# Half as many key columns in the second attention mixer: query heads in another order

## What is computed

```python
DSA_SIZES = (1024, 256, 256, 256, 32, 8)          # q, k, v, qi, ki, wi
def mixer_dsa(x, w_in, w_out):                    # x: 256 x 1024, w_in: 1024 x 1832
    q, k, v, qi, ki, wi = jnp.split(x @ w_in, DSA_SPLITS, axis=-1)
    q = q.reshape(Bn, S, 4, 4, 64)                # 16 heads of queries, 4 share one head of keys
    k = k.reshape(Bn, S, 4, 64)
    v = v.reshape(Bn, S, 4, 64)
    def block(q_b, qi_b, wi_b, bid):              # 128 positions
        rel = relu(einsum('bqhd,bsd->bqsh', qi_b, ki))
        score = einsum('bqsh,bqh->bqs', rel, wi_b) * idx_scale    # causal mask, then the top 64
        _, idx = lax.top_k(score, 64)
        logits = q_b . k[idx] / 8 - slopes[head] * distance       # masked softmax over them
        return (softmax(logits) . v[idx]).reshape(Bn, 128, 1024)
    return concat(blocks) @ w_out
```

## Time and profile before

| | |
|---|---|
| median of 3 runs | 3656.43 us (3653.99 to 3658.11) |
| the profiled execution | 3654.87 us, its span 3653.6 us |
| mean granted TensorE clock | 0.821 of full |
| PE busy over the span | 2616.1 us (72%) |
| DVE, POOL, ACT busy | 2061.5, 1516.7, 518.2 us |
| records of L1256 on BIG | 576 |

### The profile page before, as it was taken

One profiled execution on the slowest core, in us unless ns is written; L12 is line 12 of the kernel. 1 busy time (PEld: TensorE's weight loads), 2 busy tenths in 40 slices (PEclk: granted clock), 3 DMA queues, 4 the chain that ended last, 5 costly groups with the idle time before them and its releaser, 6 DMA issues.

```text
span 3653.6 us, 35023 instructions
## 1 busy us (share of the span) xinstructions
PE 2616.1 (72%) x12888; PEld 1202.7 (33%) x12888; DVE 2061.5 (56%) x5112; ACT 518.2 (14%) x1007; POOL 1516.7 (42%) x1609
## 2 busy tenths in 40 slices
PE   6688777755556865655588585556665889899998
PEld 1233222111112321111154221112312575767765
DVE  0367777656667667866404577666898354231411
ACT  1121011100012111100022110001210122020200
POOL 0035556546666666666500156666566210000000
PEclk8889888788667887767789687776867899999999
DMA  8789999999999999999822599998999786667577
GB/s 308 257 310 363 357 393 379 403 401 389 366 350 364 385 367 354 337 361 366 310 104 81 208 364 391 363 366 333 393 358 347 263 303 223 207 256 253 216 246 263
DMA packets 363672, 1156.36 MB, mean 317 GB/s; under 512 B 33712, under 2 KB 33968, under 8 KB 362476
## 3 DMA queue, kind: packets, MB, share of 16 engines
q0 software_dynamic: 232144, 849.51, 61.4%
q1 hardware_dynamic: 130940, 304.36, 23.2%
q10 hardware_dynamic: 416, 0.23, 0.0%
HBM read 1152.84 MB, written 1.15 MB: 316 GB/s over the span
## 4 chain that ended last, share of the span: by engine, by line
PE 39%; DVE 21%; DMA 20%; POOL 8%; issue 7%; another core or an unknown queue 3%; ACT 2%; SPq 0%; DVEq 0%; ACTq 0%; POOLq 0%
DMA BIG<-in_p_v_dram,IDX 12%; POOL BIG L2363 8%; PE PS L1158 8%; DVE BIG L1959 8%; PE PS L1092 7%; PE PS L1380 6%; PE PS L1362 6%; DMA BIG<-in_p_u_dram,IDX 4%; PE PS L1256 2%; PE PS L1350 2%; DMA WR<-in_w_mod_dram 1%; PE PS L1120 1%; DVE SC L2157 1%; DVE I L1883 1%
## 5 line engine op out<-in xcount | busy, mean ns | idle before, releaser
L1158 PE MATMUL PS<-BIG,DG 64*64 64x512 f32 x6144 | 1057.6, 814 | 674.0 <-DMA BIG<-in_p_v_dram,IDX 500.4
L2363 POOL DMA_INDIRECT BIG<-in_p_u_dram,IDX x768 | 735.1, 957 | 1021.4 <-ACT SCU L1525 242.5
L1959 DVE CUSTOM_DVE_ANT_0 BIG<-BIG,PS 128x1024 f32<-128x1024 f32 x768 | 927.9, 1215 | 312.7 <-DMA BIG<-in_p_u_dram,IDX 272.9
L2363 POOL DMA_INDIRECT BIG<-in_p_v_dram,IDX x768 | 738.6, 962 | 345.7 <-issue 180.4
L1158 PEld LDWEIGHTS PS<-BIG,DG 64*64 64x64 f32 x6144 | 274.4, 168 | 1342.3 <-issue 1220.1
L1092 PE MATMUL PS<-WR,HT 128*128 128x512 f32 x640 | 297.8, 619 | 10.0 <-DMA WR<-in_a_w_in_dram 4.6
L1362 PE MATMUL PS<-HT,WR 128*128 128x128 f32 x2048 | 259.8, 288 | 5.5 <-DVE mv L1807 4.9
L1362 PEld LDWEIGHTS PS<-HT,WR 128*128 128x128 f32 x2048 | 251.0, 203 | 15.5 <-issue 8.9
L1380 PE MATMUL PS<-WR,BIG 128*128 128x512 f32 x512 | 226.2, 597 | 0.0
L1092 PEld LDWEIGHTS PS<-WR,HT 128*128 128x128 f32 x640 | 123.5, 198 | 177.2 <-issue 168.5
L1380 PEld LDWEIGHTS PS<-WR,BIG 128*128 128x128 f32 x512 | 97.1, 192 | 117.4 <-issue 117.1
(11 more groups left out here) (320 smaller groups left out, 2714.0 us busy)
## 6 DMA issues: line engine op xcount, KB each, us to landing
WR<-in_mlp_w_dram SPq DMA_DIRECT2D x128, 1024.0 KB
WR<-in_w_mod_dram SPq DMA_DIRECT2D x48, 1024.0 KB
WR<-in_b_w_in_dram SPq DMA_DIRECT2D x18, 1024.0 KB
WR<-in_a_w_in_dram SPq DMA_DIRECT2D x16, 1024.0 KB
WR<-in_p_w_q_dram SPq DMA_DIRECT2D x16, 1024.0 KB
BIG<-in_dsa_w_dram POOLq DMA_DIRECT2D x16, 1024.0 KB, 7.6
BIG<-in_p_u_dram,IDX POOLq DMA_INDIRECT x768
BIG<-in_p_v_dram,IDX POOLq DMA_INDIRECT x768
```

What stands on the lines that cost most here:

```text
L1158: mm = self.e.matmul(pv[64 * i:64 * i + 64, 2 * r + n, :], dg[p, :], row[p, n * 512:n * 512 + 512], start=h == 0 and j == 0, stop=h == 7 a ...
L1959: self.e.tensor_tensor_reduce(row, row, xp, 1.0, 0.0, ALU.mult, ALU.add, m.ACTV[:, u % 4, j:j + 1]).then_inc(*self.done("dot", l, u, j))
L2363: self.e.indirect_dma_start(row, None, m.A[f"p_{table}"], bass.IndirectOffsetOnAxis(ap=m.IDX[:, u % 4, j:j + 1], axis=0)).then_inc(*m.GR.l ...
```

## The change

The 16 query heads get the order `DSA_ORDER` = 0, 4, 1, 5, 2, 6, 3, 7, 8, 12, 9, 13, ... An even place then always holds a head that uses key head 0 (or 2), an odd place one that uses key head 1 (or 3), so a tile with key head 0 on partitions 0 to 63 and key head 1 on 64 to 127 serves all of the first eight. The host permutes the query columns of `dsa_w` and the rows of `dsa_w_out_2` accordingly, and no longer repeats the keys. The keys' slab has 256 columns, its two pieces are 512 KB each, and `column` is called twice for it instead of four times. In the list of arrays of `layout` `dsa_w_out_2` moves from before `p_u` to behind `dsa_w`. The core of the diff:

```diff
+DSA_ORDER = [8 * (s // 8) + 4 * (s % 2) + s % 8 // 2 for s in range(16)]
...
-        self.side_slab(("dsa_v", b), w, 1536)
-        self.side_slab(("dsa_i", b), w, 2048, 136)
-
-    def columns(self, slab, rhs, dst, after, pace=1):
-        for i in range(4):
-            self.column(slab, i, rhs, dst, after)
+        self.side_slab(("dsa_v", b), w, 1280)
+        self.side_slab(("dsa_i", b), w, 1792, 136)
+
+    def columns(self, slab, rhs, dst, after, pace=1, count=4):
+        for i in range(count):
+            self.column(slab, i, rhs, dst, after, count)
             yield from beats(pace)
...
         for n, dst in ((2, m.d_k[:, :, b * 128:(b + 1) * 128]), (0, m.d_q[:, 0:4, :]), (1, m.d_q[:, 4:8, :])):
-            self.side_slab(("dsa", b, n), w, n * 512)
+            self.side_slab(("dsa", b, n), w, n * 512, 512 if n < 2 else 256)
             yield from beats(2)
-            yield from self.columns(("dsa", b, n), self.block_of(b), dst, ())
+            yield from self.columns(("dsa", b, n), self.block_of(b), dst, (), count=4 if n < 2 else 2)
...
-        self.e.matmul(ps[:, 0:n], m.d_q[p, h // 2, :], m.d_k[p, h // 4, 0:n], start=True, stop=True).then_inc(
+        self.e.matmul(ps[:, 0:n], m.d_q[p, h // 2, :], m.d_k[p, h // 8, 0:n], start=True, stop=True).then_inc(
...
-        m, kv = self.m, h // 4
+        m, kv = self.m, DSA_ORDER[h] // 4
...
-        self.e.scalar_tensor_tensor(lg, m.d_nd[:, 0:n], 2.0 ** (-8.0 * (h + 1) / 16), m.d_mn[:, 0:n], ALU.mult,
+        self.e.scalar_tensor_tensor(lg, m.d_nd[:, 0:n], 2.0 ** (-8.0 * (DSA_ORDER[h] + 1) / 16), m.d_mn[:, 0:n], ALU.mult,
```

More of the change, by code:

```diff
@@ L237, in __init__ @@
         self.s_end = sb("s_end", [128, 2, 16])
-        self.d_k, self.d_q = (flat[:, 1024 * i:1024 * i + 1024].rearrange("p (h t) -> p h t", h=4 + 4 * i)
-                              for i in range(2))
+        self.d_k = flat[:, 0:512].rearrange("p (h t) -> p h t", h=2)
+        self.d_q = flat[:, 1024:2048].rearrange("p (h t) -> p h t", h=8)
         self.d_score, self.d_nd, self.d_mn, self.d_ki = (flat[:, 2048 + 256 * i:2304 + 256 * i] for i in range(4))
@@ L1247, in inter, with column @@
                       skip_group_check=True).then_inc(*self.done("inter", h, j, n))
-    def column(self, slab, i, rhs, dst, after):
+    def column(self, slab, i, rhs, dst, after, count):
         m = self.m
@@ L1255, in column @@
             self.wait_ge(m.side.landed(slab, k // 4))
-            mm = self.e.matmul(ps[:, i * 128:(i + 1) * 128], self.side_of(slab, k)[:, i * 128:(i + 1) * 128], rhs(k),
+            mm = self.e.matmul(ps[:, i * 128:(i + 1) * 128], self.side_of(slab, k, count * 128)[:, i * 128:(i + 1) * 128], rhs(k),
                                start=k == 0, stop=k == 7)
         mm.then_inc(*self.done("cols", slab))
-        if i == 3:
+        if i == count - 1:
             for k in range(2):
@@ L1630, in coefficients, with column @@
         self.e.activation(x1, x1, ACT.Sin).then_inc(*self.done("sines"))
-    def column(self, slab, i, rhs, dst, after):
+    def column(self, slab, i, rhs, dst, after, count):
         m = self.m
-        if i < 3:
+        if i < count - 1:
             return
+        ps = m.PS.of("cols", slab)[:, 0:128 * count].rearrange("p (i t) -> p i t", i=count)
         self.wait_ge(m.pe.at("cols", slab))
-        self.e.activation(dst, m.PS.of("cols", slab).rearrange("p (i t) -> p i t", i=4), ACT.Copy).then_inc(
-            *self.done("cols", slab))
+        self.e.activation(dst, ps, ACT.Copy).then_inc(*self.done("cols", slab))
         m.PS.free(("cols", slab), self.done.last())
@@ L2554, in layout @@
               "b_gn_g", "b_w_out", "p_w_q", "sb_ssm_w_in_2", "ssm_w_glu_2",
-              "sb_ssm_w_out_2", "dsa_w_out_2", "ln_mix_g_2", "ln_mix_b_2", "ln_ffn_g_2", "ln_ffn_b_2",
+              "sb_ssm_w_out_2", "ln_mix_g_2", "ln_mix_b_2", "ln_ffn_g_2", "ln_ffn_b_2",
               "mlp_w1_2", "mlp_w2_2"):
@@ L2560, in layout @@
     w = a["dsa_w_in_2"][0]
-    k = np.repeat(w[:, 1024:1280].reshape(1024, 4, 1, 64), 2, axis=2).reshape(1024, 512)
+    q = w[:, 0:1024].reshape(1024, 16, 64)[:, DSA_ORDER].reshape(1024, 1024)
     ki = np.repeat(w[:, 1792:1824].reshape(1024, 1, 32), 4, axis=1).reshape(1024, 128)
-    o["dsa_w"] = c(np.concatenate([w[:, 0:1024], k, w[:, 1280:1792], ki, w[:, 1824:1832]], axis=1))
+    o["dsa_w"] = c(np.concatenate([q, w[:, 1024:1280], w[:, 1280:1792], ki, w[:, 1824:1832]], axis=1))
+    o["dsa_w_out_2"] = c(a["dsa_w_out_2"].reshape(1, 16, 64, 1024)[:, DSA_ORDER].reshape(1, 1024, 1024))
     w = np.zeros((33, 2, 512), np.float32)
```

## The result

The changed kernel has a median of 3637.38 us over 10 runs (3626.19 to 3647.97), beside 3655.21 us over 10 runs of the kernel before on the same chips (3642.96 to 3665.15). The ratio is 0.9954, with a 95% interval of 0.9938 to 0.997: 17 us faster, between 11 and 23. On another chip, where the kernel before takes 3522.98 us, a second set gave 3509.64 us, ratio 0.9961 (0.9945 to 0.9977), 13 us. The forecast was 15.2 us.

The account below looks back on a forecast made before the run. The prediction took PE to bound the tail, with gather waits ahead of it untouched. Its terms, 7.1 + 3.7 + 4.4 = 15.2 us, off the 3656.43 us median gave 3641 us, with a range from 3635 to 3650.

Parts of the forecast that it names:

- Term 1: Work removed from PE in the tail: two key column groups fewer per block, four at 1.79 us each, saving 7.1 us.
- Term 2: PE's 5.9 us of waits for the keys' slab: smaller pieces land sooner, saving 3.7 us (bounds 2.0 to 5.9).
- Term 3: PE's low clock behind the key waits: 2.8 us regained in block 0, 1.6 in block 1, together 4.4 (bounds 0 to 6.0).
- The waits cost more than their length: Step claiming that behind the key waits PE runs at 1.2 GHz instead of 2.4; low level priced at 2.8 and 3.2 us.
- The second query slab's cover: Time between that slab's landing and PE's need of it, expected to shrink from 6.9 us to over 2 us.
- Columns only: Rival: the key waits move elsewhere or stay with the clock low, so only 7.1 us is gained, 3649.3; chance 12%.
- The gathers by address: Rival: moving dsa_w_out_2 shifts the row tables and PE's gather waits grow; with 5% growth slower, 3666 us; chance 6%.
- The late slab: Rival: the second query slab lands 3.0 us late, costing 6 us per block, leaving a gain of 3, 3653; chance 7%.

Follow-up runs that it names:

- e2: Changed kernel with key pieces loaded 512 columns wide (1 MB), only 256 used, two column groups: tail 539.83 us, ratio 0.9978.
- e3: Changed kernel with each key group made twice (four groups), pieces still 512 KB: tail 543.40 us, ratio 0.999.
- e5: Changed kernel, unchanged, profiled a second time, on a second chip: tail 536.61 us, ratio 0.9961 to the kernel before.
- e7: Changed kernel with dsa_w_out_2 back in its old place in the host's list: tail 536.78 us, ratio 0.9963 to the kernel before.
- e4: Kernel before, same work; first query slab issued right behind the keys, key groups four beats behind their issue instead of two: tail 543.73 us, ratio 0.9972.
- e12: Changed kernel with the second query slab's groups begun at the beat of its issue instead of two beats behind: tail 539.36 us, ratio 0.9957.
- e11: Kernel before (512 key columns, 1 MB pieces) with key groups three beats behind their issue instead of two: tail 538.62 us, ratio 0.9975.
- e10: The kernel of e4, unchanged, profiled a second time on another chip: tail 541.90 us, ratio 0.999 to the kernel before.
- e6: Kernel before with only dsa_w_out_2 moved behind dsa_w in the host's list: tail 549.95 us, ratio 0.9999.

## Why the prediction held, and where its terms were off

**What bounds the kernel.** The tail is PE's: it is busy for about 94 to 95% of it in every profile, and groups put in or taken out moved the end by their price (e2, e3).

**Term 1, 7.1 us, is right.** There are 64 records fewer, the 32 matmuls of four groups, and e3 puts them back for 6.6 to 7.8 us.

**Term 2, 3.7 us, was too small by about one.** The landing of the first pieces was right to 0.3 us (5.1 and 4.7 against 4.95 and 4.45). Of 5.9 us of waits 1.6, 0.7 and 0.8 are left in the three profiles, so 4.3 to 5.2 are saved. What the step missed is that PE reads the keys when it gets there, and in block 0 of the first profile it got there later than computed, since the slow stretch ahead of them was longer in that execution (3.78 us for the MLP group instead of 3.46). In e5 and e7, where it was not (3.51 and 3.47), 0.5 to 0.7 us were waited there, as forecast, but the clock fell ahead of the keys of block 1 and left 0 and 0.3.

**Term 3, 4.4 us, was too large, and its reason fell.** PE's busy time is 8.2 to 10.0 us shorter, of which 7.2 are groups: the clock gave 1.0 to 2.9. A small part was the price: the prediction took 1.04 us, a row of L1079, for a half group at full clock, and rows of L1257 at 1.00 have 1.16, so its bound of 6.0 was 0.5 too high. The step that failed is "The waits cost more than their length": it read the slow groups behind the waits as caused by them. In block 1 of the first profile after it looks like that: the clock stayed up. But the order of e4 took all waits for the keys away and got 0.4 us from the clock in one execution and 3.1 in another, e2 had 2.7 us of waits in block 0 without a fall, and in e5, e7 and e3 the fall in block 1 came back as a slow group behind the first index head, and one more in the heads. That the waits have no part in it is not shown either: in all three profiles of the kernel before the clock is low behind both pairs of waits, and in e12 behind one of 1.71 us. What ties the falls to their places stays open. The kernel before shows the same slow groups, to about 0.1 us, in three executions on three chips; the order of e4 shows different ones in two; e11, which changes nothing but the beats, has 7.7 us less busy time in its one execution.

The Trainium skill, "TensorE: Matmul & The Clock Gate", Part 1, has the moment of the change depend on a free-running monitor, with other counts of slow matmuls from run to run. The pairs e4 and e10 (busy 516.48 and 513.81) and after and e5 (506.84 and 508.64) agree with that, though each pair is from two chips; the three profiles of the kernel before (516.78 to 516.87), and e5 and e7 on one chip (508.64 and 508.66), do not show it.

**The sum.** 7.2 + 4.3 to 5.2 + 1.0 to 2.9 gives, profile by profile, 13.3 to 14.5 us in the tail, against 15.2: the errors of terms 2 and 3 had opposite signs. That the sum is off by only 0.7 to 1.9 us is therefore in part luck. The 17 us measured on the first chip, with an interval from 11 to 23, agree with 13.3 to 14.5 as well as with 15.2, and cannot tell the terms apart.

**What moves.** The second query slab's cover was put at over 2 us. In block 0 the mask ran 1.9 us behind the eighth head (3162.58 to 3164.52), nearly as before, not 1.2: the MLP's square (0.69 us) was still ahead of it on DVE. POOL in order of time, block 0 and block 1 after:

```profile
3164.52 0.29 POOL L2419 TENSOR_SCALAR_AFFINE_SELECT H<-H 128x128 f32<-128x128 f32 x1 [18.33 <-DVE H L2108]
3164.98 1.52 POOL L2399 DMA_DIRECT2D BIG<-in_dsa_w_dram  x2 [0.16 <-issue]
...
3354.14 1.52 POOL L2399 DMA_DIRECT2D BIG<-in_dsa_w_dram  x2 [0.16 <-issue]
```

and the landings of its pieces (the first, then the second) in block 0, and the same in block 1:

```profile
BIG<-in_dsa_w_dram POOLq DMA_DIRECT2D x1, 1024.0 KB, 5.8
...
BIG<-in_dsa_w_dram POOLq DMA_DIRECT2D x2, 1024.0 KB, 6.7
...
BIG<-in_dsa_w_dram POOLq DMA_DIRECT2D x1, 1024.0 KB, 6.5
...
BIG<-in_dsa_w_dram POOLq DMA_DIRECT2D x2, 1024.0 KB, 7.4
```

The rows for x2 are medians of both pieces, so the second one took about 2 x 6.7 - 5.8 = 7.6 us in block 0 and 2 x 7.4 - 6.5 = 8.3 in block 1. In block 0 it landed at 3173.4, about 0.9 us before PE wanted it, in the group that began at 3173.34. In block 1, issued 0.75 us behind 3354.14, it landed at 3363.2; PE began the group at 3362.33 and wanted that piece 0.9 later, at 3363.2, and the row of that group has 2.09 us where its neighbours have 1.95. There was no cover left in that execution, and 0.14 us of that group may be a wait. This rival missed by a hair: by these numbers a mask one microsecond later would have cost about that microsecond in block 1 (an estimate).

**The rivals.** Columns only (7.1) is refuted by the tails, 13.3 to 14.5. The gathers by address are refuted by e6. The late slab did not happen, but its cover was nearly gone, as above.

## What to carry to other kernels

When a part ahead of the change varies by more than the change is worth, cut the profile at the first instruction that the change touches: the tail of the kernel before came back within 0.3 us (that of the changed one within 1.2) where whole runs spread over 22. Split the tail into PE's busy and idle time and its number of records: that separates work, waits and clock, which a list of waits does not. And before halving a transfer to remove a wait for it, try one beat more between issue and use: in the kernel before that alone took 11.5 us off in one profile (9 by the runs), where half the columns brought 13.3 to 14.5, and the two together gave the shortest tails, 532.7 and 532.8. More than half of the 11.5 is a gain in clock that was not forecast, so it is a thing to try and not one to count on.

## What the runs showed of the hardware

- The same order of work, the same records and two executions, on two chips: PE's busy time in the tail was 516.48 and 513.81 us (e4, e10). The kernel before had 516.78 to 516.87 in three, on three chips.
- Waits of 1.11 and 1.55 us left the clock at its upper level (e2, block 0); 0.50 stood behind 1.65 and 1.39 (before) and 0.57 behind 1.71 (e12, block 1); 3.28 us alone was not followed by a slow group (e11).
- A load of 512 KB with rows of 1 KB landed 5.1 and 4.7 us after its issue, beside 6.3 and 5.8 for 1 MB with rows of 2 KB and 3.4 for 272 KB with rows of 544 bytes.
- One chip ran the gathering part of the same program 130 us faster than another (the last matmul on gathered rows began at 2751.1 us in e1 and at 2883.9 before), while the tail was the same to 0.3 us.
